# Weights laid out by the host in the order of their reads, in a decoder trunk with two MoE layers

## The reference

```python
for l in range(2):
    mod = silu(c) @ ada_w[l] + ada_b[l]            # (1, 6*1024): shift, scale, gate of attention and of MoE
    if l == 0:
        h = modulate(x, sh_a, sc_a)
        proj = h @ fox_w_in[0]                     # (1024, 3*1024 + 16): q, k, v and the 16 forget gates
        logf = log_sigmoid(proj[..., 3*1024:] + fox_b_f)
        y = fox_attention(q, k, v, logf) @ fox_w_o
    else:
        kv = modulate(x, *split(silu(c) @ kv_ada_w + kv_ada_b)) @ kv_w
        y = normed(diff_attention(h @ diff_w_q, kv, lam)) @ diff_w_o
    x = layer_norm(alpha * x + (1 + g_a) * y)
    h = modulate(x, sh_f, sc_f)
    gates = top 2 of 16 experts, within the best of 4 groups     # router_w (1024, 16)
    m = sum over e of gates[:, e] * ((silu(h @ w_gate[l, e]) * (h @ w_up[l, e])) @ w_down[l, e])
    x = layer_norm(alpha * x + (1 + g_f) * m)      # w_gate, w_up: (1024, 512); w_down: (512, 1024)
```

## Time and profile before

| | us |
|---|---|
| median of 3 runs | 1034.07 (1032.99 to 1035.32) |
| the profiled execution | 1036.06 |
| its span, first to last instruction | 1033.9 |
| PE busy in the span | 927.6 (90%) |
| DVE / ACT / POOL busy | 394.7 / 203.1 / 208.0 |
| mean TensorE clock granted | 0.958 of full speed |
| read from HBM | 295.01 MB |

### The profile page before, as it was taken

How to read it: one execution, slowest core, us unless ns; L and a number is a source line. 1 busy time by engine, 2 the same in 40 slices (tenths; PEclk the granted TensorE clock), 3 DMA queues, 4 the chain that set the end, 5 groups by cost and what they waited for, 6 DMA issues and landing times.

```text
span 1033.9 us, 11337 instructions
## 1 busy us (share of the span) xinstructions
PE 927.6 (90%) x3678; PEld 453.3 (44%) x3679; DVE 394.7 (38%) x834; ACT 203.1 (20%) x422; POOL 208.0 (20%) x201
## 2 busy tenths in 40 slices
PE   4899978988899988799979998697989989989996
PEld 1587443535533333233338466444643333323332
DVE  2566786736211111111168468733511111111114
ACT  0001142201122211212210003701112222122211
POOL 3085695000230000000045062300040000000000
PEclk9899998996999999999999999988899999999999
DMA  9999965931089999859992987304029999987911
GB/s 324 382 339 387 370 213 217 422 105 61 1 357 428 426 428 431 364 237 429 414 380 84 324 294 308 131 0 163 0 99 429 429 428 428 428 356 323 429 60 41
DMA packets 63863, 296.47 MB, mean 287 GB/s; under 512 B 5804, under 2 KB 5932, under 8 KB 51544
## 3 DMA queue, kind: packets, MB, share of 16 engines
q1 hardware_dynamic: 61200, 295.71, 71.5%
q10 hardware_dynamic: 2632, 0.36, 0.2%
HBM read 295.01 MB, written 1.05 MB: 286 GB/s over the span
## 4 chain that ended last, share of the span: by engine, by line
PE 74%; DVE 12%; DMA 8%; issue 3%; SPq 2%; ACT 1%; POOLq 0%; POOL 0%; DVEq 0%; ACTq 0%
PE ps L1485 22%; PE ps L1496 11%; PE ps L1355 8%; PE ps L1503 7%; PE ps L1431 5%; PE ps L1370 5%; DMA ring<-in_ada_w_dram 4%; PE ps L1477 3%; PE ps L1311 2%; DMA ring<-in_moe_w_up_dram 2%; DMA ring<-in_moe_w_down_dram 2%; SPq L445 2%; DVE arena L904 1%; PE ps L1447 1%; PE ps L1486 1%
## 5 line engine op out<-in xcount | busy, mean ns | idle before, releaser
L1485 PE MATMUL ps<-ring,hT 128*64 128x512 f32 x560 | 255.3, 608 | 18.5 <-issue 11.4
L1486 PE MATMUL ps<-ring,hT 128*64 128x512 f32 x560 | 255.5, 608 | 0.0
L1485 PEld LDWEIGHTS ps<-ring,hT 128*64 128x64 f32 x560 | 75.5, 139 | 172.7 <-issue 169.6
L1496 PE MATMUL ps<-ring,arena 128*64 128x512 f32 x280 | 129.3, 605 | 7.6 <-DMA ring<-in_moe_w_down_dram 4.3
L1497 PE MATMUL ps<-ring,arena 128*64 128x512 f32 x280 | 129.3, 605 | 0.0
L1355 PE MATMUL ps<-hT,ring 128*128 128x256 f32 x512 | 113.3, 383 | 3.7 <-ACT hT L628 1.7
L1075 DVE TENSOR_TENSOR arena<-arena,ps 128x256 f32<-128x256 f32 x32 | 13.5, 421 | 266.0 <-ACT arena L724 157.0
L561 POOL COPY hT<-arena 128x512 f32 x32 | 19.6, 613 | 464.3 <-PE ps L1486 284.2
L1355 PEld LDWEIGHTS ps<-hT,ring 128*128 128x128 f32 x512 | 98.0, 192 | 19.7 <-issue 2.9
L371 DVE SCALAR_TENSOR_TENSOR arena<-ring,csig,arena 128x512 f32<-128x512 f32 x84 | 81.8, 973 | 3.0
L1503 PE MATMUL ps<-arena 128*128 128x512 f32 (+1 forms) x168 | 77.7, 605 | 4.2 <-DVE arena L1103 2.4
(11 more groups left out here) (278 smaller groups left out, 1031.4 us busy)
## 6 DMA issues: line engine op xcount, KB each, us to landing
ring<-in_moe_w_gate_dram SPq DMA_DIRECT2D x32, 2048.0 KB, 13.6
ring<-in_moe_w_up_dram SPq DMA_DIRECT2D x32, 2048.0 KB, 18.0
ring<-in_moe_w_down_dram SPq DMA_DIRECT2D x32, 2048.0 KB, 15.9
ring<-in_ada_w_dram SPq DMA_DIRECT2D x24, 2048.0 KB, 14.1
ring<-in_fox_w_in_dram SPq DMA_DIRECT2D x6, 2048.0 KB, 13.1
ring<-in_kv_ada_w_dram SPq DMA_DIRECT2D x4, 2048.0 KB, 12.6
ring<-in_kv_w_dram SPq DMA_DIRECT2D x4, 2048.0 KB, 17.6
ring<-in_fox_w_o_dram SPq DMA_DIRECT2D x2, 2048.0 KB, 10.3
```

Of the source, the lines that this page charges most:

```text
L1485: mg = t.matmul(ps[0:CAP, bank, :], lhs(k), wcols(ng)[:, k, :], start=(k == 0), stop=(k == KC - 1))
L1486: mu = t.matmul(ps[CAP:P, bank, :], lhs(k), wcols(nu)[:, k, :], start=(k == 0), stop=(k == KC - 1))
L1496: t.matmul(ps[0:CAP, bank, :], lhs(f), wdown(n)[:, f, 0:512], start=(f == 0), stop=(f == 3))
```

## The change

The host stores each column piece as 128 runs of 16 KB, one run for each partition, with the contents that SBUF had before. Experts are stored so that partition p receives rows p, 128+p, 256+p, ... , again one run of 16 KB. The forget-gate columns become an input of their own, `fox_w_f`, with one run of 512 bytes to a partition. With the new order of expert rows, `gather` and the transposes of `gu` and `ogu` read adjacent columns. Everything else stays: pieces, their order and their waits, the other small loads and their order, the products.

```diff
-            pieces.append(ada_dram[which][:, col:col + 512].rearrange("(k p) n -> p k n", p=P))
+            pieces.append(ada_dram[which][col // 512])
...
-            pieces.append(w[:, lo + 512 * b:lo + 512 * b + 512].rearrange("(k p) n -> p k n", p=P))
+            pieces.append(w[lo // 512 + b])
...
-                sp.dma_start(wpiece(n), pieces[n]).then_inc(full[slot(n)], 16)
+                sp.dma_start(ring[:, slot(n), :], pieces[n]).then_inc(full[slot(n)], 16)
...
-                        src = w[l, bass.ds(e, 1), :, :].rearrange("o (p k) n -> p (o k n)", p=P)
+                        src = w[l, bass.ds(e, 1), :, :].rearrange("o p n -> p (o n)")
...
-            act.dma_start(wf[:, :, :], fox_w_in[0][:, 3 * D:3 * D + HF].rearrange("(k p) n -> p k n", p=P)).then_inc(small_in, 16)
+            act.dma_start(wf[:, :, :], fox_w_f[:, :, :]).then_inc(small_in, 16)
...
-                            mm = t.matmul(ps[:, gather_bank(k), :], h[:, b, k:D:KC], pick[:, b, :],
+                            mm = t.matmul(ps[:, gather_bank(k), :], h[:, b, k * P:(k + 1) * P], pick[:, b, :],
...
-                                mm = t.transpose(ps[:, 6, q * P:(q + 1) * P], ogu[:, q:FE:4], ident[:, :])
+                                mm = t.transpose(ps[:, 6, q * P:(q + 1) * P], ogu[:, q * P:(q + 1) * P], ident[:, :])
...
-                        mm = t.transpose(ps[:, 4, f * P:(f + 1) * P], gu[:, 0, f:FE:4], ident[:, :])
+                        mm = t.transpose(ps[:, 4, f * P:(f + 1) * P], gu[:, 0, f * P:(f + 1) * P], ident[:, :])
...
+    def column_pieces(w):
+        rows, cols = w.shape
+        return w.reshape(rows // P, P, cols // 512, 512).transpose(2, 1, 0, 3).reshape(cols // 512, P, -1)
+
+    def row_pieces(w):
+        n, e, rows, cols = w.shape
+        return w.reshape(n, e, rows // P, P, cols).transpose(0, 1, 3, 2, 4).reshape(n, e, P, -1)
...
+    laid["fox_w_f"] = fox[:, main:].reshape(-1, P, fox.shape[1] - main).transpose(1, 0, 2)
```

More of the change, by code:

```diff
@@ L30, with build @@
 FAR = 1e33
-def build(nc, x, c, ada_w, ada_b, ln_attn_g, ln_attn_b, ln_ffn_g, ln_ffn_b, fox_w_in, fox_b_f, fox_w_o,
+def build(nc, x, c, ada_w, ada_b, ln_attn_g, ln_attn_b, ln_ffn_g, ln_ffn_b, fox_w_in, fox_w_f, fox_b_f, fox_w_o,
           kv_ada_w, kv_ada_b, kv_w, diff_w_q, diff_lambda, diff_norm_g, diff_w_o,
           router_w, router_b, moe_w_gate, moe_w_up, moe_w_down, out):
-    DEPTH, D, _ = ada_w.shape
+    DEPTH, D, _ = ada_w.shape[0], x.shape[2], None
     S = x.shape[1]
     NE = router_w.shape[1]
-    FE = moe_w_gate.shape[3]
+    FE = 512
     HF = fox_b_f.shape[1]
@@ L77, in build @@
     ada(0, 0, 1, 2, 3)
-    cols(N_FOXQK, fox_w_in[0], 0, 0, 1)
+    cols(N_FOXQK, fox_w_in, 0, 0, 1)
     ada(1, 0, 1)
-    cols(N_FOXQK, fox_w_in[0], 0, 2)
+    cols(N_FOXQK, fox_w_in, 0, 2)
     ada(1, 2, 3)
-    cols(N_FOXQK, fox_w_in[0], 0, 3)
+    cols(N_FOXQK, fox_w_in, 0, 3)
     ada(2, 0, 1)
-    cols(N_FOXV, fox_w_in[0], 2048, 0)
+    cols(N_FOXV, fox_w_in, 2048, 0)
     ada(2, 2, 3)
-    cols(N_FOXV, fox_w_in[0], 2048, 1)
+    cols(N_FOXV, fox_w_in, 2048, 1)
     ada(3, 0, 1, 2, 3)
     ada(4, 0, 1, 2, 3)
-    cols(N_WO[0], fox_w_o[0], 0, 0, 1)
+    cols(N_WO[0], fox_w_o, 0, 0, 1)
     experts_pieces()
@@ L97, in build @@
     ada(6, 0, 1)
-    cols(N_WQ, diff_w_q[0], 0, 0)
+    cols(N_WQ, diff_w_q, 0, 0)
     ada(6, 2, 3)
-    cols(N_WQ, diff_w_q[0], 0, 1)
-    cols(N_WO[1], diff_w_o[0], 0, 0, 1)
+    cols(N_WQ, diff_w_q, 0, 1)
+    cols(N_WO[1], diff_w_o, 0, 0, 1)
     experts_pieces()
@@ L444, in load @@
                     spent(sp, n - RING)
-                sp.dma_start(wpiece(n), pieces[n]).then_inc(full[slot(n)], 16)
-            def wpiece(n):
-                return wcols(n) if len(pieces[n].shape) == 3 else ring[:, slot(n), :]
+                sp.dma_start(ring[:, slot(n), :], pieces[n]).then_inc(full[slot(n)], 16)
             def expert_loads(l):
@@ L1562, in experts @@
                     for f in range(4):
-                        mm = t.transpose(ps[:, 5, f * P:(f + 1) * P], gu[:, 1, f:FE:4], ident[:, :])
+                        mm = t.transpose(ps[:, 5, f * P:(f + 1) * P], gu[:, 1, f * P:(f + 1) * P], ident[:, :])
                     mm.then_inc(tg_mm[1], 1)
@@ L1655, in _ @@
             spread_norm(3)
-_INS = ["x", "c", "ada_w", "ada_b", "ln_attn_g", "ln_attn_b", "ln_ffn_g", "ln_ffn_b", "fox_w_in", "fox_b_f", "fox_w_o",
+_INS = ["x", "c", "ada_w", "ada_b", "ln_attn_g", "ln_attn_b", "ln_ffn_g", "ln_ffn_b", "fox_w_in", "fox_w_f", "fox_b_f", "fox_w_o",
         "kv_ada_w", "kv_ada_b", "kv_w", "diff_w_q", "diff_lambda", "diff_norm_g", "diff_w_o",
@@ L1661, with _laid_out @@
 _OUTS = [((1, 256, 1024), "float32")]
+def _laid_out(a):
+    def column_pieces(w):
[4 more added lines that the diff above has]
+        return w.reshape(n, e, rows // P, P, cols).transpose(0, 1, 3, 2, 4).reshape(n, e, P, -1)
+    fox = a["fox_w_in"][0]
+    main = fox.shape[1] - a["fox_b_f"].shape[1]
+    laid = dict(a)
+    laid["ada_w"] = [column_pieces(w) for w in a["ada_w"]]
+    laid["kv_ada_w"] = column_pieces(a["kv_ada_w"])
+    laid["fox_w_in"] = column_pieces(fox[:, :main])
+    laid["fox_w_f"] = fox[:, main:].reshape(-1, P, fox.shape[1] - main).transpose(1, 0, 2)
+    laid["fox_w_o"] = column_pieces(a["fox_w_o"][0])
+    laid["kv_w"] = column_pieces(a["kv_w"])
+    laid["diff_w_q"] = column_pieces(a["diff_w_q"][0])
+    laid["diff_w_o"] = column_pieces(a["diff_w_o"][0])
+    for name in ("moe_w_gate", "moe_w_up", "moe_w_down"):
+        laid[name] = row_pieces(a[name])
+    return laid
 def kernel(**inputs):
@@ L1670 @@
     nc = _bacc.Bacc("TRN2", target_bir_lowering=False, num_devices=1)
+    laid = _laid_out({name: _np.asarray(inputs[name]) for name in inputs})
     arrays, args = {}, []
     for name in _INS:
-        a = _np.ascontiguousarray(inputs[name])
+        a = _np.ascontiguousarray(laid[name])
         arrays[f"in_{name}_dram"] = a
```

## The result

The changed kernel takes 1043.34 us (median of 9 runs, 1037.07 to 1044.19), the kernel before 1034.76 us (9 runs, 1032.99 to 1036.56). The ratio is 1.0078, 95% interval 1.0064 to 1.0092: slower, by 8.6 us where 7.5 were forecast. The profiled execution took 1044.19 us, its span is 1042.1. Lines of the changed kernel are numbered 3 lower from L445 on: L1352 is L1355 of before, L619 is L622, L1131's wait stands at L1128.

What follows compares the result with a forecast made beforehand. The prediction took PE as the bound, with weight landings mattering only at the start. Unit 9 8.5 us later, less 1.0 for strides, gave +7.5 us on the median 1034.07: 1041.5 us, range 1027 to 1046.

Steps and rivals of the forecast that it cites:

- Landings earlier: At the start, column pieces land sooner at 430 instead of 387 GB/s; unit 9 gains 5.4 us if nothing else is late.
- The 1.3 us: Between 18 and 28 us, q10's small packets slow q1 by 13%; this loss of 1.3 us nearly goes.
- One turn for each small packet, 16 KB or not: At the start, q10 and q1 alternate packets; 103 turns left per engine, so the small loads complete at 62.5 us.
- Which wait it ends in: In the first projection, even if ACT's issues delay modulation up to 6 us, unit 5 waits for DVE; total comes out earlier.
- rival 2: At the start, q1 pauses at 57.5 us (ACT held up or piece 10 late); unit 9 near 77.5, 1037 us; chance 0.15.
- DVE's wait: At L1131, DVE stands from about 36 until 62.5 us for the small loads, holding unit 5 until 66.7.
- Behind the wait: DVE's queued row work, copies and steps put unit 9 at 82.1 us, 8.5 us later than at 73.59.
- Strides: In gather and the transposes, adjacent reads gain 0 to 4 us, taken as 1.0 us.
- Passing the shift to the end: After unit 9, PE runs on without a stop and nothing gives the 8.5 us back.
- the sum: Whole kernel: 8.5 us lost at the start less 1.0 for strides, +7.5 us; everything else at nothing.
- the first rival: At the start, small packets don't wait one for one behind 16 KB runs; small loads complete before 50 us; 1027.7 us, chance 0.25.

Runs made afterwards that it cites:

- e2: Changed kernel with the router weights also laid out by the host, 128 runs of 512 bytes instead of 1024 of 64: 1030.42 us, ratio 0.9956 to the kernel before.
- e7: Kernel before, columns still in 2 KB runs, with only wf and the router weights laid out by the host: 1034.74 us, ratio 1.0012.
- e8: Changed kernel with wf read in 1024 runs of 64 bytes as before: 1058.37 us, ratio 1.0244 to the kernel before.
- e1: Changed kernel with ACT's first two copies out of PSUM moved before its last three small-load issues: 1046.43 us, ratio 1.0121 to the kernel before.
- e4: Kernel before with only the experts' new row order and the adjacent column reads: 1034.91 us, ratio 1.0005.
- e3: Changed kernel with each column piece in four blocks, so packets of 4 KB: 1028.49 us, ratio 0.9952 to the kernel before.
- e5: Changed kernel with both 4 KB column runs and router weights laid out by the host: 1027.06 us, ratio 0.9946 to the kernel before.

## Why the prediction was right, and where its account was not

- **Landings earlier.** Right in mechanism, too large by one term. Piece 3 was forecast "some 3.5 us" earlier, 2.0 of it from the rate and 1.3 from small packets that would no longer slow q1 (that adds up to 3.3). In e2, where nothing hides it, it is 2.3 us earlier; and e7, which takes 112 small packets from each engine and leaves the rate, brings it only 0.15 us forward. The 1.3 us were too much. Between 18 and 28 us q10 has 13.9% of the engines in the kernel before, and still 11.2% in e7 and 7.2% in e2, where the forecast let its 13% nearly go. The units begin at 37.73 (36.5 forecast), unit 9 at 70.8 (68.2 forecast, if nothing else were late). Most of the rest is a reading: 9 x 3.52 = 31.7 us was taken for units 0 to 8, but the earlier trace rows show 32.86 for them. In e2 they take 32.81, since the granted clock is 0.57 in the first 3.5 us. DVE adds the last 0.23.
- **One turn for each small packet, 16 KB or not.** Right where both queues have work, and shown by four packet lengths and by adding turns (e8) and taking them away (e2). The count of the turns was off in the changed kernel: 103 were to be left on each engine at 18 us, but 689 small packets passed by 20 us, which leaves 986, 62 to an engine on average. Even so the last small load is seen at 59.64, forecast 62.5. From 46 to 48 us 23 small packets pass beside 65 long ones, as if only some engines still had any. In e1, where 129 passed in 18 to 20 us, it is 66 beside 66 and the end is seen at 64.18.
- **Which wait it ends in.** This step failed: "ACT's own issues ... unit 5 still waits for DVE". I had seen that the hold could grow "to some 15 us" (9.23 measured for that issue, 15.8 for the last three) and dismissed it, since I priced the later modulation at no more than 6 us and took the case to come out "earlier, not later": it is rival 2, with unit 9 near 77.5, 1037 us and a chance of 0.15. Its condition came true, ACT held up and q1 empty soon after 57 us, but not its price. The first unit came 10.2 us late, 13.8 after the 36.5 that I reckoned with. ACT's copy is 8.2 us later (31.53 against 23.36), and the half clock after PE's wait adds 2.4 (1.5 on L1295, 0.9 on the two products of L1300), less the 0.3 that PE waited for piece 3 in the kernel before. With PE that late, DVE's wait was covered (unit 1's copy out at 67.44, unit 5 due at 69.58). The forecast time of 1041.5 was that of the course that e1 shows; the changed kernel came to nearly the same unit 9 (83.4, forecast 82.1) by another wait. The figure is right by luck in this part: e1, where the course is the one described, is 3 us dearer than the changed kernel.
- **Behind the wait.** In e1 the 8.5 us for unit 9 were 16.2 (89.8 against 73.59). Missing were 1.7 us of the last small load's landing, 4.4 us for the row work beside POOL, and the low clock: unit 5 takes 6.6 us there instead of 3.5. Half of that came back, since DVE's steps on piece 6 took 6.0 us with POOL done, and not the 8.0 taken.
- **Strides.** 1.0 us taken, 0 to 4 as bounds; e4 shows none, and its interval leaves room for 0.4 us at most.
- **Passing the shift to the end.** The v products are 9.7 us late, the end of the span 8.2 (1042.1 against 1033.9). What was given back goes with PE's granted clock, which is not the same in each kernel's profiled execution. From the first product of L1431 to the first of L1477 (before) and in the same stretch after and in e3:

```profile
198.50:260.50 62.00, 55.25 (x149) 29.89 (x148) 33.36 (x90) 8.14 (x15) 2.03 (x5) 0.83 0.32 127
```

```profile
207.10:267.50 60.40, 53.15 (x150) 28.78 (x148) 32.09 (x81) 8.15 (x15) 2.03 (x5) 0.86 0.37 144
```

```profile
192.30:249.60 57.30, 49.24 (x149) 25.39 (x147) 32.11 (x81) 8.14 (x15) 2.03 (x5) 0.91 0.39 152
```

The same products take 62.0, 60.4 and 57.3 us at a granted clock of 0.83, 0.86 and 0.91. The stretch ahead of it, from the first v product on, before and in e5:

```profile
102.71:198.52 95.81, 86.22 (x358) 43.36 (x357) 71.09 (x150) 28.25 (x88) 55.11 (x37) 0.96 0.80 295
101.67:194.31 92.64, 83.35 (x358) 42.71 (x358) 70.09 (x150) 28.25 (x88) 55.25 (x37) 1.00 0.73 293
```

So e5, 1.0 us ahead at the first v product, is 4.2 ahead at L1431 and 8.9 at L1477 (251.59 against 260.53), and its span ends 9.0 earlier. The start, all that the sum counts beside the strides, explains 1.0 of them. The ten runs of e2 go the same way: its three fastest (1025.47 to 1026.17 us) have a mean clock of 0.958 to 0.959, the slowest (1034.10) 0.950. Why the clock is granted differently was not tried and stays open. Whether the longer runs bring it about is open too, and so is whether e5 beats e2 and e3.

By the Trainium skill ("DMA: Bandwidth & Descriptors", Queues, rings and completion order) an engine drains a whole packet of several descriptors from one queue before it switches; this made the first rival. It is not what these runs show where q1 fills the engines: in 22 to 24 us the counts stay equal or nearly so at 4, 8 and 16 KB. The 689 beside 52 in 18 to 20 us can't decide it, as q1's share was down to 79.3%.

## What to carry to other kernels

Before making the packets of a bulk stream longer, look at what else uses the DMA engines at that time: a small load needs as many turns as it has runs, and each turn lasts one packet of the stream. Lay out the small inputs first, or leave the stream at 4 KB: both gave a time 0.4 to 0.5% below the kernel before, where 16 KB alone lost 0.8%. And follow a slow queue to the engine that issues on it: here the issuer was held before any consumer of the data. Last, check with the end of the span what a gain at the start is worth: in its profiled execution e5 gained 1.0 us there and 9.0 in all.

## What the runs showed of the hardware that was not expected

- An issue of 8 KB held its engine for 9.23 us (22.01 in e8), while the runs issued before it were still queued.
- The pace of one for one between two queues held from 2 KB to 16 KB while the long packets filled the engines (not in 18 to 20 us of the changed kernel, 689 beside 52); in 22 to 24 us the engines moved 0.80 MB of 16 KB packets beside 51 small ones, and 0.68 MB of 2 KB packets beside 334.
- After a wait of 10.45 us the granted clock was 0.50 for 4 us, after one of 15.73 us it was 0.57 over the next 7.2 us.
- Beside POOL's TENSOR_TENSOR of L375 a DVE instruction of 64 x 512 took up to 1.50 us instead of 0.42 (e1, from 64.18 on; POOL's ran from 64.14 to 65.40).
- With the same products, the stretch from the first v product to L1431 took 95.8 us at a granted clock of 0.96 and 92.6 at 1.00.
